# A block of two transformer layers on one NeuronCore: TensorE's two outer loops written out

## The reference

```
# first block
proj = rmsnorm(x) @ w_in                  # 2048 x 5120, then pooling and a gated scan
x = x + rmsnorm(mix @ w_out)              # 2048 x 2048
ff = square(relu(rmsnorm(x) @ w_mlp_in)) @ w_mlp_out      # 2048 x 8192 x 2048: "the MLP"
x = x + rmsnorm(ff)
# second block, with shift, scale and gate vectors m from silu(c) @ ada_w + ada_b  (2048 x 12288)
z = gelu(n @ a_w_in); u, v = split(z)     # 2048 x 8192
x = x + m2 * ((u * spatial(rmsnorm(v))) @ a_w_out)        # 4096 x 2048
g, v = split(dwconv(n @ w_up)); x = x + m5 * ((silu(g) * v) @ w_down)   # 2048 x 11264, 5632 x 2048: "the FFN"
out = rmsnorm(x)
```

## Time and profile before

| | us |
|---|---|
| median of 3 runs | 2573.86 |
| lowest, highest | 2572.02, 2575.58 |
| the profiled execution, its span | 2572.2 |
| PE busy | 2494.5 (97%) |
| PEld busy | 2437.4 (95%) |
| DVE busy | 1682.6 (65%) |
| ACT busy | 1154.8 (45%) |
| POOL busy | 100.1 (4%) |
| chain that ended last: share of PE | 92% |
| chain that ended last: "issue" | 2% |

### The profile page before, as it was taken

How to read it: one execution, slowest core, us unless ns; L and a number is a source line. 1 busy time by engine, 2 the same in 40 slices (tenths; PEclk the granted TensorE clock), 3 DMA queues, 4 the chain that set the end, 5 groups by cost and what they waited for, 6 DMA issues and landing times.

```text
span 2572.2 us, 50625 instructions
## 1 busy us (share of the span) xinstructions
PE 2494.5 (97%) x19544; PEld 2437.4 (95%) x19544; DVE 1682.6 (65%) x1941; ACT 1154.8 (45%) x1344; POOL 100.1 (4%) x71
## 2 busy tenths in 40 slices
PE   8999998999999999998999999998999999999998
PEld 7989997999999999997888999998999999999997
DVE  6784767776675765776866876655666556655665
ACT  5554544543543543543544533434544344443443
POOL 0330011000000000001000000000000000000000
PEclk9999998999999999998999999999999999999999
DMA  6434453776777776774787776454555555555553
GB/s 224 140 132 164 141 194 109 299 274 253 260 278 254 257 278 251 257 273 168 262 312 259 271 279 237 158 187 151 184 180 174 194 173 181 182 184 180 187 181 123
DMA packets 151486, 542.88 MB, mean 211 GB/s; under 512 B 17712, under 2 KB 20016, under 8 KB 151216
## 3 DMA queue, kind: packets, MB, share of 16 engines
q1 hardware_dynamic: 151344, 540.81, 59.8%
HBM read 538.64 MB, written 2.10 MB: 210 GB/s over the span
## 4 chain that ended last, share of the span: by engine, by line
PE 92%; DVE 4%; issue 2%; ACT 1%; DMA 1%; POOL 0%; DVEq 0%; SPq 0%; ACTq 0%
PE bank L340 28%; PE bank L341 27%; PE bank L342 27%; PE bank L356 2%; PE bank L357 2%; PE bank L358 2%; PE mis L420 1%; DVE acc L1022 1%; DMA raw<-wstream 1%; DVE wlo L969 1%; PE mis L524 1%; DVE rstd L1015 0%; PE bank L377 0%; PE mis L401 0%; ACT whi L575 0%
## 5 line engine op out<-in xcount | busy, mean ns | idle before, releaser
L969 DVE TENSOR_TENSOR wlo<-raw,whi 128x1024 fp32r<-128x1024 f32 x824 | 1011.1, 1236 | 717.2 <-ACT whi L575 712.7
L575 ACT ACTIVATE whi<-raw 128x1024 fp32r<-128x1024 f32 x824 | 861.3, 1056 | 1093.8 <-PE bank L342 794.2
L340 PE MATMUL bank<-xs,whi 128*128 128x256 f32 x3456 | 986.9, 286 | 33.1 <-issue 13.1
L341 PE MATMUL bank<-xs,whi 128*128 128x256 f32 x3456 | 983.4, 285 | 0.0
L342 PE MATMUL bank<-xs,wlo 128*128 128x256 f32 x3456 | 983.3, 285 | 0.0
L340 PE MATMUL bank<-hs,whi 128*128 128x256 f32 x2496 | 707.8, 284 | 0.0
L341 PE MATMUL bank<-hs,whi 128*128 128x256 f32 x2496 | 706.3, 283 | 0.0
L342 PE MATMUL bank<-hs,wlo 128*128 128x256 f32 x2496 | 706.3, 283 | 0.0
L340 PEld LDWEIGHTS bank<-xs,whi 128*128 128x128 f32 x3456 | 669.4, 194 | 36.0 <-issue 28.7
L341 PEld LDWEIGHTS bank<-xs,whi 128*128 128x128 f32 x3456 | 669.4, 194 | 0.3 <-issue 0.2
L342 PEld LDWEIGHTS bank<-xs,wlo 128*128 128x128 f32 x3456 | 669.0, 194 | 0.0
(11 more groups left out here) (153 smaller groups left out, 1058.9 us busy)
## 6 DMA issues: line engine op xcount, KB each, us to landing
raw<-wstream SPq DMA_DIRECT2D x824, 512.0 KB, 4.4
aring<-astream SPq DMA_DIRECT2D x192, 512.0 KB, 4.6
x<-xT SPq DMA_DIRECT2D x4, 512.0 KB, 5.6
outT<-acc SPq DMA_DIRECT2D x4, 512.0 KB, 2.7
pw<-poolw SPq DMA_DIRECT2D x1, 1024.0 KB, 9.2
ws<-wsT SPq DMA_DIRECT2D x8, 128.0 KB, 4.2
bs<-bsp SPq DMA_DIRECT2D x8, 128.0 KB, 4.6
mk<-masks SPq DMA_DIRECT2D x1, 288.0 KB, 8.5
```

The source lines that it names most:

```text
L340: pe.matmul(o, whi[:, slot, c], h, start=st, stop=False, skip_group_check=True)
L341: pe.matmul(o, whi[:, slot, c], l, start=False, stop=False, skip_group_check=True)
L575: act.activation(whi[:, slot, :], raw[:, slot, :], ACT.Copy).then_inc(hi_ready, 1)
L969: dve.tensor_tensor(wlo[:, slot, :], raw[:, slot, :], whi[:, slot, :].bitcast(F32), ALU.subtract).then_inc(lo_ready, 1)
```

## The change

The two outer loops of TensorE's program become loops of Python, so their bodies stand in the program four times and twice, with the index as a constant. The inner loops stay loops at run time.

```
-            with pe.Fori(0, 4) as q:
+            for q in range(4):
                 with pe.Fori(0, 2) as p:
                     for a in range(2):
                         group(q * 8 + p * 2 + (G_MLP + a), xs, 2 * a, wait=xs0(1))
...
-            with pe.Fori(0, 2) as c:
+            for c in range(2):
                 with pe.Fori(0, 4) as p:
                     for a in range(2):
                         group(c * 12 + p * 2 + (G_FF + a), xs, 2 * a, wait=xs0(3))
```

## The result

| | before | after |
|---|---|---|
| median, us | 2574.15 | 2552.33 |
| lowest, highest | 2572.02, 2575.58 | 2550.05, 2553.66 |
| span of the profiled execution | 2572.2 | 2551.9 |
| PE busy | 2494.5 | 2486.8 |

The account below looks back on a forecast made before the run. PE was taken to bound the kernel (busy 2494.5 of 2572.2 us). Standstills of 16.50 and lower-clock excess of 5.81 made 22.31 us, so 2573.86 - 22.3 = 2551.6 us, range 2547 to 2557, at 85%.

Parts of the forecast that it names:

- The bound and the four places: PE bounds the kernel; its four taken outer branches, three in the MLP and one in the FFN, cost 22.31 us together.
- The clock: First units after the four edges (and one second unit) run slow at the lower granted clock; excess 5.81 us.
- The cover: At the MLP's turns no other engine is late behind the standstill; DVE's split of the fifth unit has 4.9 us to spare.
- The join at 1590: Inside the mixing part, two loops written one after the other, same transposes and 2.48 us reduction: PE's matmuls show no gap.
- Entries, straight code, register operations: Added inner-loop entries, longer straight code and removed register operations count for nothing; 1.2 us for entries kept for the range.
- The cause: Long outer branches (L503 median 5867 ns, L544 4054) are code fetched again; what differs from L504 is how far back they go.
- The gap as a wait for the split: Rival: PE waits for lo_ready in the MLP rounds' fifth to eighth unit, taking back up to 13.6 us: 2565; 6%.
- the FFN's gap as a wait for DVE: Rival: the FFN's gap is DVE's x at L1083, no branch, so 3.2 us stay: 2554.8; 4%.
- That PE stands at the turn for the register-valued waits: Rival: branches weren't the cause; PE stands at a round's turn for something else such as these waits: 2573.9; 2%.
- misses of the inner branches at new places: Slower rival: moved inner loops of MLP and FFN straddle pages, ways back cost 49.6 us less 22.3 gained: 2601; 3%.
- The total: Profiled execution 2572.2 - 22.3 = 2549.9; median of runs 2573.86 - 22.3 = 2551.6 us.

Follow-up runs that it names:

- dve_late3: The changed kernel with three additional DVE subtractions ahead of the reduction at the turns of MLP rounds 2, 3 and 4; 2552.11 us.
- dve_late6: The changed kernel with six additional DVE subtractions ahead of the reduction at the turns of MLP rounds 2, 3 and 4; 2564.07 us.
- all_out: The kernel before with all of TensorE's loops written out, inner ones too; 2551.13 us, ratio to before 0.9900.
- ffn_slot0: The kernel before with the FFN's outer loop kept and its head placed at the start of a page, so a round touches 7 pages; 2571.54 us.
- ffn_slot224: The kernel before with the FFN's outer loop kept and its head at place 224 of a page, so a round touches 8 pages; 2575.42 us.
- apart4: The changed kernel with the FFN's inner xs loop drawn apart by four jumped-over stretches, so its way back goes over 7 pages; 2553.74 us.
- apart5: The changed kernel with the FFN's inner xs loop drawn apart by five jumped-over stretches, so its body touches 8 pages; 2587.14 us.
- mlp_only: The kernel before with only the MLP's outer loop written out, the FFN's kept a loop; 2551.67 us, ratio to before 0.9904.
- ffn_only: The kernel before with only the FFN's outer loop written out, the MLP's kept a loop; 2570.47 us, ratio to before 0.9978.
- compact: The kernel before, outer loops kept and placed at page starts, MLP's hs groups made an inner loop, transposes behind it; 2551.13 us, ratio to before 0.9906.

## Why the prediction was right

**The bound and the four places.** Right, within 0.02 us: 6.05, 5.98, 7.10 and 3.18 us were worked out, 6.05, 5.98, 7.09 and 3.20 came. A standstill on the engine that bounds the kernel, behind which every other engine has run out of things to do, is worth its full length.

**The clock.** Right: it was 5.8 of the 22.3. It is easily left out, since no list of waits has it; it stands in the granted clock of the windows behind the gap, and in the page as PE's busy time.

**The cover.** Right: 4.9 us worked out, 4.54 measured, and dve_late3 (3.4 us later, nothing paid) and dve_late6 (6.8 us later, paid) bracket it. The join at 1590 was the better half of the argument.

**Entries, straight code, register operations.** Nothing, as taken; all_out says the same of the inner branches.

**The cause.** Right in kind: the branch waits for its code. Wrong in the rule. The prediction held length to be what differs between L504 and L544, and set aside the page "Runtime: NRT & Kernel Launch" of the Trainium skill ("Instruction fetch mechanics") with both its figures. One of them, 2,048 instructions or eight pages of 256 for PE, fits what ffn_slot0, ffn_slot224, apart4 and apart5 measure, once one counts pages touched instead of instructions and leaves one for the page brought ahead. The other, a window of two pages, is against what they show: the way back of apart4 goes over seven pages in 0.2 us. 1,584 instructions are 6.2 pages: seven or eight, by where they begin. The step that failed is the reading that by 2,048 instructions the FFN's branch would be free, and that its 4.05 us therefore spoke against this figure: it is free or not by where the loop lies (0.21 us in ffn_slot0 and mlp_only, 3.89 in ffn_slot224). The forecast didn't suffer, since it priced the branches from their own rows.

**The rivals.** The gap as a wait for the split and the FFN's gap as a wait for DVE: both out, by the trace after and by ffn_only. That PE stands at the turn for the register-valued waits is out as well: compact keeps them and has no standstill there. Of the slower rival, misses of the inner branches at new places, the trace shows none in after; its 3% was more luck than argument in its reasons, but the rule now gives the ground: a body of 788 touches four or five pages wherever it lies. For the FFN's round it was the real thing: had only the MLP been written out, 3.2 us more hung on where the FFN's loop came to lie, and it came to lie well.

**The total.** 2551.6 forecast, 2552.33 measured, from a sum for the profiled execution (2549.9) that came out at 2551.9. The 2 us are bouts of the lower clock and short waits elsewhere, inside the allowance made for them.

## What to carry to other kernels

Look at the sequencer's own rows, branch by branch: a way back that takes 4 to 6 us instead of 0.2 has lost its code, and costs the standstill that it leaves on the bounding engine plus the time at the lower clock behind it. Before writing a loop out, count the pages of 256 instructions that a round touches, in the assembled program (a weight load and its matmul are two, and waits count too): on TensorE here, without a hint, seven are free and eight are not, so shortening a round with an inner loop, or placing its head at the start of a page, gets the same time. And since any code ahead moves a loop, a change far from it can switch such a wait on or off; compare the branch rows before crediting the change.

## What the runs showed of the hardware that was not expected

- Without a hint, whether the way back is free depends on the pages touched: 7 pages 0.21 us (ffn_slot0), 8 pages 3.89 us (ffn_slot224), with the same instructions.
- A prefetch hint at the head of a round of 2,398 instructions shortens the branch from 5.87 to 4.07 us and doesn't remove it. In the same kernel the branch of the FFN's round, 4.05 us in before, took 0.23 us.
- A body that touches eight pages loses more than its way back: its forward jumps wait too, up to 4.4 us, and 33 us came of one more jump over unused places (apart4, apart5).
- The lower clock followed the standstills of 2.3 and 2.7 us at two turns of dve_late6, not the third of 2.3, while one of 2.9 us, the FFN's edge in before, wasn't followed by it. What decides between them, no run shows.
